# A two-block network on one core: an early sum for the convolution's norm, a root's spread between two half products, and an earlier split of two weight slots

## What is computed

```python
def conv_module(u_val, u_gate, conv_w, conv_b, ln_g, ln_b, w_proj):
    a = u_val * jax.nn.sigmoid(u_gate)
    ...
        feature_group_count=CONV_WIDTH) + conv_b
    a = jax.nn.silu(layer_norm(a, ln_g, ln_b))
    return a @ w_proj
...
        hc = xi @ w1[e] + b1[e]
        g, u = hc[:, :D_EXPERT], hc[:, D_EXPERT:]
        g = jnp.minimum(g, SWIGLU_LIMIT)
        u = jnp.clip(u, -SWIGLU_LIMIT, SWIGLU_LIMIT)
        hm = (u + 1.0) * (g * jax.nn.sigmoid(SWIGLU_ALPHA * g))
        return hm @ w2[e] + b2[e]
```

```python
    n_f = head_group_norm(y_f).reshape(B, S, RET_V_WIDTH).astype(g_f.dtype)
    n_b = head_group_norm(y_b).reshape(B, S, RET_V_WIDTH).astype(g_b.dtype)
    return jax.nn.silu(g_f) * n_f + jax.nn.silu(g_b) * n_b
...
    y_attn = windowed_gqa(q_a, k_a, v_a, sink_logits) @ w_o_attn
    y_ret = bidirectional_retention(q_r, k_r, v_r, g_f, g_b, decay_fwd, decay_bwd) @ w_o_ret
    merged = gates[..., :D_MODEL] * y_attn + gates[..., D_MODEL:] * y_ret
    return merged @ w_out
```

## Time and profile before

| | before |
|---|---|
| runs | 2387.15, 2385.66, 2385.75 us; median 2385.75 us |
| profiled execution | 2387.82 us, its span 2386.1 us |
| TensorE busy | 2259.8 us, 95% of the span |
| VectorE, ScalarE, POOL busy | 729.7, 621.8, 395.5 us |
| chain that ended last | TensorE 67%, DMA 13%, SP's queue 11%, VectorE 6%, issue 2%, ScalarE 1% |
| traffic | 688.63 MB, mean 289 GB/s |
| TensorE's mean granted clock | 0.977 |

### The profile page before, as it was taken

One profiled execution on the slowest core, in us unless ns is written; L12 is line 12 of the kernel. 1 busy time (PEld: TensorE's weight loads), 2 busy tenths in 40 slices (PEclk: granted clock), 3 DMA queues, 4 the chain that ended last, 5 costly groups with the idle time before them and its releaser, 6 DMA issues.

```text
span 2386.1 us, 34777 instructions
## 1 busy us (share of the span) xinstructions
PE 2259.8 (95%) x13114; PEld 1391.4 (58%) x13115; DVE 729.7 (31%) x1365; ACT 621.8 (26%) x901; POOL 395.5 (17%) x371
## 2 busy tenths in 40 slices
PE   7999899999999999999997999999999989999897
PEld 5877744444444444444446998899898853333333
DVE  4854322222222222222235244212324341111013
ACT  2142111111111111111214670443368011111111
POOL 2000000000000000000004751688486000000000
PEclk9999899999999999999998999999999979999999
DMA  9963399999999999989993533565354456999651
GB/s 361 379 242 106 89 383 418 418 418 418 418 418 418 418 418 418 418 335 417 418 392 106 159 107 106 177 194 176 108 177 124 167 222 245 373 406 397 275 238 70
DMA packets 223482, 688.63 MB, mean 289 GB/s; under 512 B 28330, under 2 KB 117362, under 8 KB 187570
## 3 DMA queue, kind: packets, MB, share of 16 engines
q1 hardware_dynamic: 221776, 685.82, 75.0%
q10 hardware_dynamic: 1490, 1.61, 0.2%
q0 software_dynamic: 144, 0.20, 0.0%
HBM read 686.53 MB, written 1.05 MB: 288 GB/s over the span
## 4 chain that ended last, share of the span: by engine, by line
PE 67%; DMA 13%; SPq 11%; DVE 6%; issue 2%; ACT 1%; POOL 0%; ACTq 0%; DVEq 0%; POOLq 0%
PE PS L1040 16%; DMA RAW<-in_w_exp_in 9%; PE PS L691 9%; SPq L458 7%; PE PS L1142 6%; PE PS L680 6%; PE PS L665 6%; PE PS L1004 4%; PE PS L1153 3%; PE PS L1342 3%; SPq L480 3%; DMA W<-in_w_ada 3%; PE PS L1023 2%; PE PS L735 1%; PE PS L777 1%
## 5 line engine op out<-in xcount | busy, mean ns | idle before, releaser
L1040 PE MATMUL PS<-RAW,Z 128*64 128x512 f32 x3168 | 713.6, 597 | 23.2 <-DMA RAW<-in_w_exp_in 23.1
L400 POOL TENSOR_TENSOR WLO_D<-W,WHI_D 128x512 fp32r<-128x512 f32 x284 | 361.5, 1309 | 1183.9 <-ACT WHI_D L396 1133.5
L1040 PEld LDWEIGHTS PS<-RAW,Z 128*64 128x64 f32 x3168 | 213.8, 137 | 454.2 <-issue 376.5
L1142 PE MATMUL PS<-W,Z 128*64 128x512 f32 (+1 forms) x1056 | 215.3, 564 | 10.8 <-DMA W<-in_moe_w 10.2
L691 PE MATMUL PS<-Z,W 128*128 128x256 f32 x768 | 170.5, 382 | 7.3 <-DVE Z L2317 5.8
L396 ACT ACTIVATE WHI_D<-W 128x2048 fp32r<-128x2048 f32 x71 | 135.3, 1908 | 119.1 <-DMA W<-in_ffn_w 47.4
L691 PEld LDWEIGHTS PS<-Z,W 128*128 128x128 f32 x768 | 146.7, 192 | 29.4 <-issue 5.1
L1142 PEld LDWEIGHTS PS<-W,Z 128*64 128x64 f32 x1056 | 75.1, 138 | 151.3 <-issue 131.9
L1004 PE MATMUL PS<-Z 128*128 128x64 f32 x1088 | 128.6, 278 | 0.0
L1004 PEld LDWEIGHTS PS<-Z 128*128 128x128 f32 x1088 | 127.4, 196 | 0.4 <-issue 0.4
L2080 DVE TENSOR_TENSOR Z<-Z,PS 128x1024 f32<-128x1024 f32 x66 | 80.4, 1218 | 125.9 <-PE PS L1023 125.9
(11 more groups left out here) (402 smaller groups left out, 2738.3 us busy)
## 6 DMA issues: line engine op xcount, KB each, us to landing
RAW<-in_w_exp_in SPq DMA_DIRECT2D x256, 1024.0 KB, 19.2
RAW<-in_w_exp_out SPq DMA_DIRECT2D x128, 1024.0 KB, 21.7
W<-in_moe_w SPq DMA_DIRECT2D x128, 704.0 KB, 15.3
W<-in_w_in SPq DMA_DIRECT2D x52, 1024.0 KB, 5.4
W<-in_moe_w SPq DMA_DIRECT2D x40, 1024.0 KB, 15.9
W<-in_ffn_w SPq DMA_DIRECT2D x33, 1024.0 KB, 5.3
W<-in_w_ada SPq DMA_DIRECT2D x24, 1024.0 KB, 14.6
W<-in_w_out SPq DMA_DIRECT2D x12, 1024.0 KB, 5.2
```

Of the source, the lines that this page charges most:

```text
L400: i = eng.tensor_tensor(lo[:, c:c + 512], raw[:, c:c + 512], hi[:, c:c + 512].bitcast(F32), ALU.subtract)
L1040: mm = pe.matmul(ps(bank, 512, 64 * h, 64 * h + 64), x, w[:, c:c + 512], start=first, stop=final, skip_group_check=True)
L1142: mm = pe.matmul(o if b < 2 else o.rearrange("p (i n) -> p i n", i=2), X1[:, s, :], rhs, start=(s == 0), stop=(s == 7), skip_group_check=True)
```

## The change

It has three parts. In turn 7 of the attention's loop VectorE waits for the taps and writes the one element ahead of the wait for head 7's exponentials. In both mixers TensorE's fourth half job of the attention's output product moves behind the spread, and VectorE gates that half behind the products of the heads. In the last chunk of the first expert stage ScalarE splits its two slots behind the second product, ahead of the hidden values' copy; an added one-element copy behind that copy signals `m1_split_room`, for which POOL waits before its first lo part.

```diff
@@ -586,6 +586,8 @@
                 for q in range(q0, q0 + 11):
+                    if q == 0:
+                        pool.wait_ge(sem("m1_split_room"), 1)
                     if q == 2:
                         pool.wait_ge(sem("normed"), 8)
                     split_dense(pool, q)
@@ -1296,8 +1298,7 @@
                 mm.then_inc(sem("norm_sum"), 1)
-                for part in range(2):
-                    feature_job(lin, 1, z(QA, QA + 4), 4, part)
+                feature_job(lin, 1, z(QA, QA + 4), 4, 0)
 
                 pe.wait_ge(sem("pool_tables"), l + 2)
                 norm[0] += 1
@@ -1309,6 +1310,7 @@
                         if i:
                             mm.then_inc(sem("norm_sum"), 1)
+                feature_job(lin, 1, z(QA, QA + 4), 4, 1)
                 for s in range(2):
@@ -1560,13 +1562,16 @@
                 def chunk(g, split=None):
                     turned(g)
+                    if split:
+                        act.wait_ge(sem("m1_group_done"), g * 12 + 2)
+                        split()
                     act.wait_ge(sem("m1_group_done"), g * 12 + 8)
                     act.activation(HS1[:, 0:512], ps(0), ACT.Copy).then_inc(sem("m1_hs_act"), 1)
+                    if split:
+                        act.activation(SPARE[:, :], ONES[:, 0:1], ACT.Copy).then_inc(sem("m1_split_room"), 1)
                     act.wait_ge(sem("m1_gate_part"), g + 1)
                     act.activation(SIG1, GPART, ACT.Sigmoid, scale=1.702).then_inc(sem("m1_sig"), 1)
                     tokens(g + 2)
-                    if split:
-                        split()
                     act.wait_ge(sem("m1_group_done"), g * 12 + 12)
@@ -1926,16 +1931,16 @@
                     taps(2)
+                    if i == 7:
+                        assert conv[0] == TAPS
+                        dve.wait_ge(sem("tap"), 4 * TAPS)
+                        dve.tensor_copy(GS[:, 16:17], GS[:, 0:1]).then_inc(sem("norm_in"), 1)
                     dve.wait_ge(sem("exp_done"), h + 1)
                     normalise(h, (P, T))
                 if i >= 2 and i % 2 == 1:
                     p = (i - 3) // 2
                     dve.wait_ge(sem("values_done"), 2 * p + 2)
                     dve.tensor_copy(Z[:, (UG + p) * T:(UG + p + 1) * T], ps(7, T, c0=(p % 2) * T)).then_inc(sem("pair_copied"), 1)
-                if i == 7:
-                    assert conv[0] == TAPS
-                    dve.wait_ge(sem("tap"), 4 * TAPS)
-                    dve.tensor_copy(GS[:, 16:17], GS[:, 0:1]).then_inc(sem("norm_in"), 1)
                 if i == 8:
@@ -2307,7 +2312,7 @@
                 inverse_root(SQ[:, 0:T], ps(4, T), HD).then_inc(sem("norm_in"), 1)
-                gated(lin, G2A, (2, 3))
+                gated(lin, G2A, (2,))
                 for p in range(2):
@@ -2316,6 +2321,7 @@
                     link(i)
                     dve.tensor_tensor(z(QR + 2 * p, QR + 2 * p + 2), H[:, 2 * p:2 * p + 2, :], H[:, 2 * p + 4:2 * p + 6, :],
                                       ALU.add).then_inc(sem("ret_out"), 1)
+                gated(lin, G2A, (3,))
                 lin = lins[f"wo_ret{l}"]
```

## The result

The changed kernel takes 2371.63 us (median of four runs, 2370.47 to 2378.2) against 2386.4 for the kernel before: a ratio of 0.9944, 95% interval 0.9925 to 0.9962. The prediction was 2371.5 us. The total agrees; what follows shows that two of its three parts do not, and that their errors cancel. How close it came is chance: timed again in five runs, the same kernel took 2375.55 us.

What follows compares the result with a forecast made beforehand. TensorE's chain, with its waits for VectorE and the clock lost behind them, was taken as the bound. Terms 3.6 + 3.1 + 3.1 + 1.7 + 1.5 + 2.1 = 15.1 us, 14.25 off the median: 2371.5 us, range 2366 to 2378.5.

Steps and rivals of the forecast that it cites:

- Part 1: Head 7 of block one's attention: early one-element copy starts the second convolution sum near 202.7 instead of 206.33, 3.6 us.
- the slow sum: Head 7's convolution sum, 3.50 us against 1.99 for a like sum, mostly at 1.2 GHz; 1.5 us expected back.
- The step that passed the gain through the weight stream: Expert stage: the whole weight stream starts with the first chunk and moves with it, so part 1's gain passes in full.
- the first of the rivals: Expert stage: the weight stream swallows part 1, price 3.6 us, giving 2375 us; chance 0.05.
- Part 2, the order: Mixer ends: spread ahead of the fourth half, TensorE goes on at 1452.4 instead of 1455.49; 3.1 us in each mixer.
- Part 2, the clock: Mixer 0: without TensorE's wait the 1.7 us of lost clock should return, bounds 0 and 1.7; counted by half.
- Part 3: First expert stage's last chunk, early split: 4.0 - 2.5 = 1.5 us, plus 2.1 us of clock.
- the delay: Last chunk's gating: two clamps and two products slowed by 2.75 us beside POOL, 2.5 after slack; ends 0 and 5.2.
- The fall of the clock in the new wait: Last chunk: TensorE's clock falling in its new wait, 1.7 us, counted only in the worst end of the range.
- the clock's return behind the updates: Behind the last chunk's updates of X: between 0 and 4.2 us of clock won back, half taken, 2.1 us.
- The second rival: Last chunk: POOL shuts VectorE out until it is through; part 3 becomes -9.3 us, total 2384.4, no change; chance 0.06.
- the third, a clock that does not recover: First chunks of the expert stage, 303 to 523 us, stay at 1.2 GHz; slower from 19 us, 2401.5 at 30; chance 0.03.

Runs made afterwards that it cites:

- the run without it: Kernel before with TensorE's new mixer order alone, VectorE still gating the fourth half ahead of its products of the heads: 2388.59 us, ratio 1.0009.
- part 2 alone: Kernel before with only the spread put between the two last half products and VectorE's gating moved, in both mixers: 2376.25 us, ratio 0.9959.
- the run with TensorE kept busy: Kernel before with four unread 128x256 matmuls added in TensorE's wait for VectorE's heads at the end of both mixers: 2383.18 us, ratio 0.9984.
- two half passes: Early split alone, POOL's first lo part let go behind the fifth product, the second behind the next chunk's token copy, against the kernel before: 2381.92 us, ratio 0.998.

## Why the prediction was right, and where not

**Part 1** was right: 3.6 us predicted, 3.7 in the trace, 3.5 by the run that has it alone. One step of it was luckier than it looks: the 1.5 us of the slow sum were counted in full from one trace, and two of six traces of the old order do not lose them, which leaves some 3.2. The step that passed the gain through the weight stream held too: 1040 us of that stage kept their length, and the first of the rivals fell.

**Part 2, the order**, was right in each step: the spread ahead of the fourth half, no wait of TensorE for the heads, 3.1 us in each mixer (3.2 by the trace, 32.36 us against 35.57). That VectorE's half of the move is needed follows from the run without it.

**Part 2, the clock**, is the term that was mis-sized. I took 1.7 us in mixer 0, counted it by half, since it "need not be in every one", and nothing in mixer 1, on the strength of one trace in which mixer 1 kept its clock. Four executions of the old order show mixer 0 losing 1.6 to 1.7 every time and mixer 1 in three of four, up to 2.9; keeping TensorE busy without any other change brings 3.9. So part 2 is 10.5 us, not the 7.05 that stood in the sum for the median. The time of part 2 alone would not show that (7.05 is inside its 6.7 to 12.9 us); the chains do, and the run with TensorE kept busy, whose 1.7 to 6.0 us lie above the 0.85 that was counted.

**Part 3** is the step that failed: 3.6 us predicted, 0.3 measured, no different from nothing (ratio 1.000). The place of the delay was right, and its size: 2.75 us for the four operations predicted, 3.0 measured (0.75 + 0.35 + 0.95 + 0.94), 2.80 us of waiting against 2.5. Two terms were not. The fall of the clock in the new wait was put into the range and not into the sum; it came in all three executions seen, 1.6 to 1.7 us. And the clock's return behind the updates, 2.1 us, was measured against the one trace at hand, where the 24 sums took 8.37 us; with the old split they take 7.12 to 8.37 in five traces, 7.6 on average, and with the early one 7.1, so that there was little more than the 0.9 us of the four sums ahead of them to win. 3.9 - 2.8 - 1.6 + 0.9 + 0.6 = 1.0 us is left by the traces, and the time cannot tell that from nothing.

That the delay came out at its size is in part luck. The prediction took means for prices, and the means are of two kinds of instruction. The eight updates of the earlier trace rows, taken one at a time, take 1.48 to 1.49 us five times, in turn with POOL's pieces, and 0.47 to 0.59 three times; the three products of the earlier trace rows take 1.68, 1.66 and 0.70. So a product that meets POOL costs more than the 0.7 us taken, and the second clamp, which came late in one of POOL's pieces, less than its 0.9. Two of POOL's pieces in the changed kernel:

```profile
1249.22 1.44 POOL L400 TENSOR_TENSOR WLO_D<-W,WHI_D 128x512 fp32r<-128x512 f32 x1
...
1250.62 1.71 POOL L400 TENSOR_TENSOR WLO_D<-W,WHI_D 128x512 fp32r<-128x512 f32 x1
```

The first ends at 1250.66, and the product that began at 1249.57 ends 0.55 us later; the second ends at 1252.33, and the product that began at 1251.24 ends 0.54 us later. The two clamps end 0.28 us behind the end of the piece that was under way when they began. The prediction's reading of its rows, slowing and not standing still, is thus the wrong one: each operation stands until the piece under way is through.

The Trainium skill, SBUF — State Buffer, "Who interferes with whom", has VectorE's instruction blocked for the whole of the GpSimd instruction that has the port first. The trace agrees: the four operations were 0.35 to 0.95 us longer and not the length of a whole piece (11.12 / 8 = 1.39), because each piece had begun before the operation did. The kinds of operation are as the page says: L2118 in the changed kernel, one operand in PSUM, took 0.68 us beside POOL as without it.

The sum came out by luck, because the errors cancel: part 2 is 3.5 us above what stood in it, part 3 is 3.3 below. The second rival, POOL shutting VectorE out until all of its pieces are through, did not occur; nor did the third, a clock that does not recover: it is 1.00 from 303 to 523 us in the changed kernel too.

## What to carry to other kernels

Work that is moved out of one engine's way lands beside something else: before moving a POOL pass over SBUF, list VectorE's operations with all operands in SBUF at the new place, and look for a stretch in which it has none; here two half passes fit where one whole pass gave everything back. Price such a meeting from single instructions, not from the mean of a row. A wait of TensorE of 2 to 3 us costs its own length and often the clock behind it (1.1 to 2.9 us here, and nothing in some executions), so count both, and read the clock's part from several executions, not from one. Where a wait cannot be removed, a few idle matmuls in it can be worth more than they cost.

## What was not expected of the hardware

The same instructions behind the same wait took 27.03, 28.16, 29.86 and 29.89 us in four executions: whether and for how long the clock is lost differs from one execution to the next. The kernel before took between 2382.41 and 2392.73 us in 29 runs, a spread as wide as most of the effects studied here. That it is the sum of many such waits is not shown; the mean granted clock goes with it, 0.978 in the fastest run and 0.974 in the slowest, with a correlation of -0.60 over the 29. And useless work can shorten an execution: eight matmuls that nobody reads, four in each mixer, took 3.9 us off.
